# Value stage of a PEER layer: dense rows in three pair buffers, gathered rows in four and then six, the row list copied by ScalarE

## What is computed

```python
def peer_ffn(x, wq, subkeys, u, v):
    ...                                    # per token: 8 heads x 16 experts of 16384, with weights g
    def tok_fn(args):
        xc, ec, gc = args
        act = jax.nn.gelu(jnp.einsum('td,tkd->tk', xc, u[ec]), approximate=False)
        return jnp.einsum('tk,tkd->td', gc * act, v[ec])
```

## Time and profile before

| | us |
|---|---|
| runs (3), median | 1818.73 |
| runs, lowest and highest | 1818.67, 1825.79 |
| profiled execution, its own time | 1826.05 |
| profiled execution, span from first to last instruction | 1824.2 |
| what lies around the span | 1.85 |
| value stage, first to last of its matmuls in the trace | 1225.0 to 1713.5 |

### The profile page before, as it was taken

One profiled execution on the slowest core, in us unless ns is written; L12 is line 12 of the kernel. 1 busy time (PEld: TensorE's weight loads), 2 busy tenths in 40 slices (PEclk: granted clock), 3 DMA queues, 4 the chain that ended last, 5 costly groups with the idle time before them and its releaser, 6 DMA issues. The chain is left out here.

```text
span 1824.2 us, 23200 instructions
## 1 busy us (share of the span) xinstructions
PE 1281.4 (70%) x7315; PEld 1156.4 (63%) x7315; DVE 1459.3 (80%) x1969; ACT 787.8 (43%) x1348; POOL 824.8 (45%) x824
## 2 busy tenths in 40 slices
PE   7999999999993350000212212299999999999997
PEld 6999999988983340000111111278999999989886
DVE  5334555664378999999999999889999999989855
ACT  4334445654211112000566666684444444434554
POOL 1100000000144455555555555288878888888303
PEclk9999999999997675555555555599999999999999
DMA  7974444457499999999999999919999999999852
GB/s 236 292 240 139 139 142 148 147 202 255 154 422 422 421 408 408 409 403 417 409 408 409 410 400 410 423 40 378 372 370 369 366 374 372 361 329 370 332 196 105
DMA packets 157684, 575.04 MB, mean 315 GB/s; under 512 B 14548, under 2 KB 72229, under 8 KB 121648
## 3 DMA queue, kind: packets, MB, share of 16 engines
q0 software_dynamic: 58544, 362.96, 50.0%
q1 hardware_dynamic: 99072, 211.20, 33.2%
HBM read 569.89 MB, written 7.36 MB: 316 GB/s over the span
## 5 line engine op out<-in xcount | busy, mean ns | idle before, releaser
L1492 DVE SCALAR_TENSOR_TENSOR rows<-rows,banks 128x2048 f32<-128x2048 f32 x208 | 466.7, 2278 | 21.6 <-DMA rows<-peer_u_dram,expert 21.5
L694 POOL DMA_INDIRECT rows<-peer_u_dram,expert x208 | 197.4, 949 | 412.0 <-DVE rows L1492 179.8
L740 POOL DMA_INDIRECT vrow<-peer_v_gathered_dram,vidx x224 | 337.7, 1508 | 73.3 <-issue 39.5
L2026 PE MATMUL banks<-hot,hot 128*128 128x128 f32 x512 | 103.3, 367 | 237.4 <-ACT hot L1079 233.5
L2026 PEld LDWEIGHTS banks<-hot,hot 128*128 128x128 f32 x512 | 89.1, 263 | 251.9 <-issue 178.8
L794 ACT CAST whi<-raw 128x2048 fp32r<-128x2048 f32 x80 | 152.4, 1905 | 174.1 <-PE banks L1767 92.3
L1594 DVE SCALAR_TENSOR_TENSOR hres<-vrow,slot_coef,hres 128x672 f32<-128x672 f32 x224 | 204.6, 913 | 13.8 <-DMA vrow<-peer_v_gathered_dram,vidx 13.3
L1608 DVE TENSOR_TENSOR vlo<-vraw,vhi 128x1376 fp32r<-128x1376 f32 x128 | 202.7, 1584 | 3.5 <-ACT vhi L1129 3.3
L2053 PE MATMUL banks<-vhi,chi 128*128 128x460 f32 x762 | 181.8, 374 | 3.0 <-ACT vhi L1129 3.0
L2060 PE MATMUL banks<-vlo,chi 128*128 128x460 f32 x762 | 180.5, 372 | 3.5 <-DVE vlo L1608 3.4
L1258 DVE TENSOR_TENSOR wlo<-raw,whi 128x2048 fp32r<-128x2048 f32 x46 | 106.0, 2305 | 92.2 <-ACT whi L794 91.0
(11 more groups left out here) (277 smaller groups left out, 2967.8 us busy)
## 6 DMA issues: line engine op xcount, KB each, us to landing
vraw<-peer_v_dense_dram SPq DMA_DIRECT2D x128, 688.0 KB, 7.2
raw<-w_in_dram SPq DMA_DIRECT2D x48, 1024.0 KB, 5.7
raw<-w_out_dram SPq DMA_DIRECT2D x16, 1024.0 KB, 5.4
wqraw<-peer_wq_packed_dram SPq DMA_DIRECT2D x16, 1024.0 KB, 9.0
raw<-ple_gate_dram SPq DMA_DIRECT2D x16, 1024.0 KB, 5.5
vrow<-peer_v_gathered_dram,vidx POOLq DMA_INDIRECT x224, 7.5
rows<-peer_u_dram,expert POOLq DMA_INDIRECT x208, 13.4
bias_by_distance<-bias_of_heads POOLq DMA_DIRECT2D x1, 3072.0 KB, 12.8
```

Of the source, the lines that this page charges most:

```text
L694: pool.indirect_dma_start(dst[:, :], None, peer_u[0], bass.IndirectOffsetOnAxis(ap=expert[b][:, k:k + 1], axis=0))\
L740: pool.indirect_dma_start(vrow[j][:, :], None, v_gathered, bass.IndirectOffsetOnAxis(ap=idx[:, j % TT, j // TT:j // TT + 1], axis=0))\
L1492: dve.scalar_tensor_tensor(out=r[:, :], in0=r[:, :], scalar=1.0, in1=xps[tt][:, :], op0=ALU.mult, op1=ALU.mult, accum_out=dots[b][:, k:k + ...
L2026: last = pe.matmul(bank[SPREAD_BANK[m]][:, a * P:(a + 1) * P], hot2[tt][m][:, a, :], hot1[tt][m][:, a, :], start=True, stop=True)
```

## The change

The value stage is laid out anew; what is computed, and the number of matmuls, vector operations and gathers, stay the same.

- **Dense rows** come in pairs of chunks: three buffers `vpair` of 2 x 1376 numbers for each partition, so 64 loads of 1376 KB in place of 128 of 688 KB. The host lays `v`'s dense columns out so that each partition's 11008 bytes of a pair lie together. A pair is loaded once PE is through with both chunks of the pair three pairs back. The third pair buffer lies at 16 KB, over `pp_keep`; its first load waits for `pp_out`. The loop body is now 6 chunks (`VBODY`), 21 turns and a tail of 2.
- **Gathered rows** have four buffers in the first turn and six afterwards. Buffers 4 and 5 lie over the part of `spread` that the first six chunks use. So a gather waits until DVE has used the rows of two chunks earlier in the first turn (and for the first two chunks of the second), and of three chunks earlier from then on.
- **Row numbers** are copied by ACT, two chunks at a time, into three `vidx` (L725 on POOL goes). The first two copies stand ahead of ACT's copy of `tsl[1]`, the others behind `vhi` of every second chunk.
- **The gate stage's first loads** wait for `clo` of `NKEYS - 4` = 124 chunks as before; the last dense load ahead of them on SP now waits for 122 chunks of PE in place of 124.

```diff
-VRING = 4
-VROWS = 8
-VBODY = 8
+VPAIRS = 3
+VBODY = 2 * VPAIRS
+VROWS0, VROWS = 4, 6
...
+    o_pair = [176 * KB, 176 * KB + 8 * VDENSE, 16 * KB]
+    vpair = [at(f"vpair{b}", o_pair[b], [P, 2 * VDENSE]) for b in range(VPAIRS)]
+    vraw = [vpair[r // 2][:, r % 2 * VDENSE:(r % 2 + 1) * VDENSE] for r in range(VBODY)]
...
+            v_load(0, 0)
+            v_load(1, 1)
+            sp.wait_ge(pp_sb, 8 + TT)
+            sp.wait_ge(eaten, PEER_STEPS * TOPK)
+            sp.dma_start(ppdram, pp_keep[:, :, :]).then_inc(pp_out, 16)
+            sp.wait_ge(pp_out, 16)
+            v_load(2, 2)
             with sp.Fori(1, V_TURNS) as i:
-                for r in range(VBODY):
-                    sp.wait_ge(v_lo_mm, VBODY * i + r - VRING + 1)
-                    v_load(VBODY * i + r, r)
-
-            sp.wait_ge(clo_ready, NKEYS - VRING)
+                for b in range(VPAIRS):
+                    sp.wait_ge(v_lo_mm, VBODY * i + 2 * b + 2 - VBODY)
+                    v_load(VPAIRS * i + b, b)
+            sp.wait_ge(v_lo_mm, VBODY * V_TURNS + 2 - VBODY)
+            v_load(VPAIRS * V_TURNS, 0)
+
+            sp.wait_ge(clo_ready, NKEYS - 4)
             stream("gate", NG["gate"])
...
+            def v_fetch(turn, i, pairs=VPAIRS):
+
+                for p in range(pairs):
+                    pool.wait_ge(vidx_ready, VPAIRS * i + p + 1)
+                    pool.nop(nofuse=True)
+                    for j in range(2 * TT):
+                        n = 2 * TT * p + j
+                        b = n % (VROWS0 if turn == 0 else VROWS)
+                        if j % TT == 0:
+                            if turn == 0 and n == FIRST_OVER_HOTS[0]:
+                                pool.wait_ge(spread_sb[1], SPREADS)
+                            if turn == 0 and n >= VROWS0:
+                                pool.wait_ge(v_used, n + TT - VROWS0)
+                            elif turn == 1 and n < VROWS0:
+                                pool.wait_ge(v_used, TT * VBODY + n + TT - VROWS0)
+                            elif turn == 1 and n < VROWS:
+                                pool.wait_ge(clo_ready, VBODY)
+                            elif turn >= 1:
+                                pool.wait_ge(v_used, TT * VBODY * i + n + TT - VROWS)
+                            pool.nop(nofuse=True)
+                        pool.indirect_dma_start(vrow[b][:, :], None, v_gathered,
+                                                bass.IndirectOffsetOnAxis(ap=vidx[p][:, j % TT, j // TT:j // TT + 1], axis=0))\
+                            .then_inc(fetched[b], 16)
...
+            act.wait_ge(routed, PEER_STEPS)
+            for p in range(2):
+                act.copy(vidx[p][:, :, :], by_tile[:, :, 2 * p:2 * p + 2]).then_inc(vidx_ready, 1)
             act.wait_ge(tsl_mm[1], 1)
...
+            def indices_ahead(i, r):
+
+                act.wait_ge(v_used, TT * (VBODY * i + r - 1))
+                v_index(i + (r + 3) // VBODY, (r + 3) % VBODY // 2)
...
+    v_pairs = v[:, VGATH:].reshape(NKEYS // 2, 2, P, VDENSE).transpose(0, 2, 1, 3).reshape(NKEYS // 2, P, 2 * VDENSE)
```

More of the change, by code:

```diff
@@ L221, in build @@
     o_spread = [190 * KB, 160 * KB]
-    tsl = [at("tsl0", 198 * KB, [P, 3, P]), at("tsl1", 201 * KB, [P, 3, P])]
+    tsl = [at(f"tsl{t}", 198 * KB, [P, 3, P]) for t in range(TT)]
     hot1 = [[at(f"hot1_{t}_{b}", o_spread[t] + 2 * b * KB, [P, TOKB, NKEYS]) for b in range(HOTS[t])]
@@ L304, in build @@
     ssqs = place("ssqs", [P, TT, D // CHUNK_C])
-    vidx = [place(f"vidx{r}", [P, TT, VBODY // 2], i32) for r in range(2)]
+    vidx = [place(f"vidx{p}", [P, TT, 2], i32) for p in range(VPAIRS)]
+    by_tile = slot_row[:, :].rearrange("p (t s) -> p t s", t=TT)
     assert base + cursor[0] <= nc.sbuf_usable_end, (base + cursor[0], nc.sbuf_usable_end)
@@ L764, in _ @@
                     weigh_hots(i, m)
-            v_index(0, 0)
             pool.wait_ge(pp_out, 16)
-            v_fetch(0, 0, first=True)
-            v_fetch(0, 1)
-            with pool.Fori(1, V_TURNS - 1) as i:
-                v_fetch(i, 0)
-                v_fetch(i, 1)
-            v_fetch(V_TURNS - 1, 0, last=True)
-            v_fetch(V_TURNS - 1, 1, last=True)
+            for turn in range(2):
+                v_fetch(turn, turn)
+            with pool.Fori(2, V_TURNS) as i:
+                v_fetch(2, i)
+            v_fetch(2, V_TURNS, pairs=V_TAIL // 2)
             pool.wait_ge(clo_ready, NKEYS)
@@ L1616, in _ @@
                     v_lows(i, r)
+            for r in range(V_TAIL):
+                v_lows(V_TURNS, r)
             for b in range(VBLK):
@@ L2059, in v_products @@
                         dst, cols = v_block(tt, b)
-                        last = pe.matmul(dst, chi[r % 2][:, tt, :], vlo[r % VRING][:, cols], start=False, stop=False,
+                        last = pe.matmul(dst, chi[r % 2][:, tt, :], vlo[r][:, cols], start=False, stop=False,
                                          skip_group_check=True)
@@ L2078, in _ @@
                     dst, cols = v_block(tt, b)
-                    for n, (x, v) in enumerate(((chi, vhi[r % 2]), (clo, vhi[r % 2]), (chi, vlo[r % VRING]))):
+                    for n, (x, v) in enumerate(((chi, vhi[r % 2]), (clo, vhi[r % 2]), (chi, vlo[r]))):
                         last = pe.matmul(dst, x[r % 2][:, tt, :], v[:, cols], start=False, stop=n == 2,
```

101 lines of the change are left out of this document (47 added, 54 removed).

## The result

| us | before | after |
|---|---|---|
| median of the runs beside each other (4 and 4) | 1819.55 | 1911.34 |
| lowest and highest | 1818.67, 1825.79 | 1904.98, 1919.72 |
| ratio, with 95% interval | | 1.0492 [1.0466, 1.0517] |
| span of the profiled execution | 1824.2 | 1910.1 |

A forecast was written before the change was run, and what follows sets the result against it. PE's pace of 3.76 us a chunk was taken as the bound; 5.3 + 0.7 + 1.0 - 0.7 = +6.3 us on the median of 1818.7 gave 1825.0 us, with an 8-in-10 range of 1816 to 1843.

The forecast's parts named there:

- What bounds the kernel before: Value stage: PE is always busy and sets 3.76 us a chunk; better supply can win some 7 us.
- Part 1, the first turn: Four row buffers at the stage's start: PE stalls in chunks 4 to 7, +5.3 us, plus 0.7 for PE's clock.
- Part 2, six buffers: Gathers after the first turn: 7.66 us there against 7.4 to landing; +1.0 us, bounds 0 to +20.
- Part 3: Dense rows loaded in pairs of chunks: the longer load stays hidden, 0 us, bounds 0 to +3.
- rival A: Whole stage: pairs' longer runs slow gathered rows' landing by 0.9 us on average, pace 3.8 to 4.0; 1847 us, chance 0.30.
- Part 4: Row numbers copied by ACT instead of POOL: 0 us, down to -5.4 if late stalls came of POOL falling behind.
- Part 5, the end: End of the value stage: gate loads go out some 7 us sooner; -0.7 us, bounds -1.2 to +2.
- B: Gather issues on POOL held up by DVE's two-input operations: two more stalls of 5.4 us, 1835 us, chance 0.08.

The follow-up runs named there:

- b_rows12: Kernel before with row numbers copied by ScalarE, bodies of 12 chunks, and twelve row buffers instead of eight from chunk 12 on: 1819.2 us, ratio 0.9980.

## Why the prediction was wrong

- **What bounds the kernel before** was read rightly: PE at its pace, some 7 us to be won at most, and all of the later loss had to come from supply. b_rows12, with no wait for a row behind chunk 3, is 0.2% faster. The pace itself had a little room: both kernels with six dense places and eight row buffers ran at 3.73 us from chunk 16 on, in place of 3.76. ScalarE never waited for dense rows there and waited 5.0 us in 14 places in the kernel before; that this is the difference isn't shown.
- **Part 1, the first turn**: right in mechanism and place. It was to come 6.0 us late at chunk 7, PE stood 3.51 us there, 1.90 and 1.17 us before that, and the next matmuls ran at 2.51 and 2.02 us in place of 1.41. Predicted 5.3 + 0.7, measured 8.6; an issue of 2.71 us in place of 0.95 stands ahead of the longest wait, 1.8 us more, and accounts for most of the difference.
- **Part 2, six buffers** is the step that failed: +1.0, with +20 as the upper end, and it is 66.7 us after and 47 us with single loads alone. The step said "7.66 us are there, against 7.4 to landing". The room of 7.66 counted from an issue 0.30 us after DVE's end; behind a real wait it is 0.78, so 7.66 + 0.30 - 0.78 = 7.18. The 7.4 was that of an issue of 0.96 us; behind a real wait the first issue of a chunk took 2.25 us on the average (51 cases), and one of 2.7 us moves the landing by 1.8. The working then corrected for being late ten times by 0.3 us, where being late is the state in which the next issue is long: behind a wait 2.25 us, otherwise 1.28.
- **A row was misread** under that step, and the row read rightly already gives the loss that single loads show. `vrow_last` is the eighth buffer, so the gather at 1302.90 ends a chunk, and the two behind it, at 1304.30 and 1306.75, are the first and the second of the next chunk:

```profile
1302.90 1.10 POOL L740 DMA_INDIRECT vrow_last<-peer_v_gathered_dram,vidx  x1 [0.16 <-POOL vidx L725]
1304.30 2.14 POOL L740 DMA_INDIRECT vrow<-peer_v_gathered_dram,vidx  x1 [0.31 <-DVE hres L1594]
```

  The DMA view of that one issue at 1304.30, with the us to landing as its last number, reads the same for the one at 1308.02:

```profile
vrow<-peer_v_gathered_dram,vidx POOLq DMA_INDIRECT x1, 8.2
```

  The gather of 0.96 us and 7.4 to landing is thus a *second* one, issued 4.2 us behind the row that released it. First ones take 2.0 to 2.2 us in the quiet state (2.13 at 1308.02) and landed after 8.2 us, those at 1304.30 and 1308.02 both. A first one behind a real wait needs 0.78 + 8.2 = 9.0 us from the end of DVE's row, and 7.66 + 0.30 = 7.96 are there: 1.0 short, a third of it for each chunk, so a pace of 4.1 us before any pairs. That is an estimate from these rows; single loads with six buffers measured 4.15 and 4.17.
- The parts fit together roughly. With T the pace, three chunks of lead give a room of 7.18 + 3 (T - 3.76). Short issues and single loads need 0.95 + 6.0 = 6.95: room enough, and the pace measured is 3.80. Pairs need 0.95 + 7.3 = 8.25, so T = 4.1 (measured 3.96). Single loads with first issues of 1.8 us on the average behind a wait need 7.7: T = 3.9 (4.15). Pairs with such issues of 2.25 need 9.5: T = 4.5 (4.39). These are estimates from means, off by up to 0.25 us. They put the best and the worst of the four kernels right, and the two between them the wrong way round: 3.9 against 4.1 by the estimate, 4.15 against 3.96 measured.
- **Part 3**: right that the pairs' own landing is hidden. Wrong to close the part there: a load can be hidden and still delay another queue's. That was in rival A, with 0.9 us; it is 1.3, and 31 us of the 92. Rival A also took the gathers' runs for 2688 bytes each: the traces record their data as packets of 5376 bytes, two rows in one, beside 5504 or 11008 of the dense loads.
- **Part 4**: within its range, 0 down to -5.4, measured -4 (with the longer loop body).
- **Part 5, the end**: predicted -0.7, measured +8.1 in the profile. The gate's loads did go out early, at 1771.33. Overlooked was what follows them on POOL: its remainder of the gate weights came early too, and met DVE's last work.
- **Rivals.** A had 0.30 and 1847, B 0.08 and 1835, each as if it came alone. What happened is both, on the same ring that was taken to have 0.26 us to spare. A's signs came (waits for gathers all over the stage), and its time didn't: the pace was 4.39 and not 3.8 to 4.0. B was priced as two more stalls, "POOL meets DVE in the same phase every time" was written there and not carried to its end: every time means again and again, in 55 of 256 issues. Alone it is worth 53 us with pairs and 47 with single loads, and the range should have held it.

## What to carry to other kernels

Where a buffer's release, the request and the landing form a ring, price the ring in its *starved* state: the wake-up behind a real wait, and the issue in the phase into which the wait puts it, both read from the few places in the trace where the ring already failed (here, 3.19 us, and not the steady 0.96). Make sure first which turn of the ring a row belongs to, by counting buffers: here the quiet rows alone had much of the answer, once the first gather of a chunk was told from the second. If the room less the need is under one such issue, the loss is not a stall now and then but one that returns every few chunks, and so a new pace. And when something is made to come earlier, follow what it releases on every engine, since an engine that was idle can now run beside one that it holds up.

## What the runs showed of the hardware

- An indirect gather's issue on GpSimd (128 rows of 2688 bytes) took 0.95 us while VectorE stood and up to 2.7 to 3.2 us beside VectorE instructions with two operands in SBUF that followed each other (55 of 256 in the kernel after); with one operand of the longest of them in PSUM none of 256 took over 2.5 us, and the mean was 1.06.
- A wait of GpSimd for a VectorE instruction ended 0.78 us after that instruction in all nine kernels with one wait a chunk in which I measured it (before, after and seven of the experiments: medians 0.77 or 0.78); the gap between two of its own issues was 0.30.
- Beside GpSimd's `tensor_tensor` of 128x2048, both of them with two operands in SBUF, VectorE's of 1.58 us became 5.89 beside one of 5.11, and a row operation of 0.91 became 5.22 beside one of 5.41; apart they took 1.58, 0.91 and 4.61. VectorE's instruction started second each time and ended 1.44 and 0.71 us after GpSimd's.
- Loads with 11008 bytes in a run lengthened the landing of gathered rows of 2688 bytes from 5.9 to 7.3 us, with the DMA engines 88% busy at 320 GB/s, below the 378 of the kernel before. As two transfers with 5504 bytes in a run, issued together, they made it 6.3 us.
